# A seventh weight slot for the experts, laid over the constant tables

## The reference

```python
def first_block(x, c, ...):
    ...                                     # attention and gated linear attention
    h = rms_norm(x, g_pre_ffn[l]) * (1.0 + scale2) + shift2
    y = moe_ffn(h, router_w[l], router_b[l], w_gate_up[l], b_gate_up[l], w_down[l], b_down[l])
    return x + gate2 * rms_norm(y, g_post_ffn[l])

def moe_ffn(h, router_w, router_b, w_gate_up, b_gate_up, w_down, b_down):
    logits = (xt @ router_w + router_b).astype(jnp.float32)
    top_v, top_i = lax.top_k(logits, TOP_K)            # 4 of 32 experts for each token
    gates = jax.nn.softmax(top_v, axis=-1)
    ...
    gu = xb @ w_gate_up[e] + b_gate_up[e]               # 1024 x 2048 for each expert
    act = x_glu * jax.nn.sigmoid(SWIGLU_ALPHA * x_glu) * (x_lin + 1.0)
    return act @ w_down[e] + b_down[e]                  # 1024 x 1024 for each expert
```

## Time and profile before

| | us |
|---|---|
| median of 3 runs | 2546.22 |
| lowest, highest | 2543.89, 2552.05 |
| the profiled execution | 2542.5 |
| its span | 2540.5 |
| TensorE busy | 2288.7 (90%) |
| VectorE busy | 872.3 (34%) |

### The profile page before, as it was taken

One profiled execution on the slowest core, in us unless ns is written; L12 is line 12 of the kernel. 1 busy time (PEld: TensorE's weight loads), 2 busy tenths in 40 slices (PEclk: granted clock), 3 DMA queues, 4 the chain that ended last, 5 costly groups with the idle time before them and its releaser, 6 DMA issues. The chain is left out here.

```text
span 2540.5 us, 25065 instructions
## 1 busy us (share of the span) xinstructions
PE 2288.7 (90%) x9740; PEld 1310.2 (52%) x9740; DVE 872.3 (34%) x1800; ACT 416.9 (16%) x897; POOL 106.9 (4%) x74
## 2 busy tenths in 40 slices
PE   7999999888898888888879998898789999989998
PEld 4555343333333333333337677655648764647873
DVE  5665222111121122221236434654567301343201
ACT  1222110111111111111122321112321001222100
POOL 1000000000000000000000000000200000000000
PEclk8999999999999999999989999989989999999999
DMA  9766588999989999999977711465246543423441
GB/s 327 272 234 232 195 307 320 412 409 408 372 312 413 412 404 409 409 411 398 402 303 273 262 62 49 171 246 213 100 141 240 188 159 122 161 89 119 165 153 46
DMA packets 212253, 655.47 MB, mean 258 GB/s; under 512 B 8518, under 2 KB 13182, under 8 KB 195540
## 3 DMA queue, kind: packets, MB, share of 16 engines
q1 hardware_dynamic: 208368, 647.86, 67.2%
q0 software_dynamic: 1712, 3.60, 0.4%
q10 hardware_dynamic: 2004, 1.67, 0.2%
HBM read 652.05 MB, written 1.05 MB: 257 GB/s over the span
## 5 line engine op out<-in xcount | busy, mean ns | idle before, releaser
L1599 PE MATMUL ps<-w,XE 128*64 128x512 f32 x1536 | 365.9, 632 | 61.0 <-DMA w<-in_w_gate_up 57.5
L807 PE MATMUL ps<-HF,w 128*128 128x256 f32 x1408 | 309.6, 383 | 1.8 <-DVE CF L2897 1.8
L807 PEld LDWEIGHTS ps<-HF,w 128*128 128x128 f32 x1408 | 270.3, 192 | 41.6 <-issue 4.5
L1599 PEld LDWEIGHTS ps<-w,XE 128*64 128x64 f32 x1536 | 123.5, 145 | 289.0 <-issue 287.4
L1629 DVE TENSOR_TENSOR T<-ps,BB 128x512 f32<-128x512 f32 x64 | 44.3, 692 | 615.5 <-PE ps L1599 615.5
L625 DVE SCALAR_TENSOR_TENSOR AUX<-w,CS,AUX 128x512 f32<-128x512 f32 (+1 forms) x228 | 169.8, 745 | 8.1
L823 PE MATMUL ps<-w,AF 128*128 128x512 f32 x352 | 151.6, 593 | 1.8 <-DVE AF L2919 1.8
L807 PE MATMUL ps<-HT,w 128*128 128x256 f32 x640 | 148.2, 391 | 5.5 <-DVE dqk L2338 3.7
L1670 PE MATMUL ps<-GR,AT 128*64 128x512 f32 x256 | 121.3, 630 | 30.5 <-DMA AUX<-in_w_down 29.8
L823 PE MATMUL ps<-w,HT 128*128 128x512 f32 (+1 forms) x352 | 146.7, 571 | 0.3 <-DVE S L1444 0.3
L1670 PE MATMUL ps<-w,AT 128*64 128x512 f32 x512 | 119.9, 611 | 20.1 <-DMA w<-in_w_down 16.8
(11 more groups left out here) (580 smaller groups left out, 2570.3 us busy)
## 6 DMA issues: line engine op xcount, KB each, us to landing
w<-in_w_gate_up SPq DMA_DIRECT2D x96, 2048.0 KB, 15.8
w<-in_w_down SPq DMA_DIRECT2D x32, 2048.0 KB, 19.4
w<-in_ada_w SPq DMA_DIRECT2D x24, 2048.0 KB, 8.0
w<-in_ffn_w_in SPq DMA_DIRECT2D x20, 2048.0 KB, 8.0
w<-in_w_in SPq DMA_DIRECT2D x17, 2048.0 KB, 9.7
GR<-in_w_gate_up SPq DMA_DIRECT2D x16, 2048.0 KB, 18.2
AUX<-in_w_gate_up SPq DMA_DIRECT2D x16, 2048.0 KB, 23.0
GR<-in_w_down SPq DMA_DIRECT2D x16, 2048.0 KB, 10.1
```

What stands on the lines that cost most here:

```text
L807: ins = e.matmul(out_, w[:, k, c:c + n], HT[:, k, :], start=k == 0, stop=k == kc - 1, skip_group_check=True)
L1599: ins = e.matmul(b[j * n:j * n + n, :], FM.XE[:, side(x), 4 * kh + k, j * n:j * n + n], ring.tile(512, 1024, "gu", ex_, h, kh, x[0])[:, k, ...
```

## The change

A third region becomes a weight slot in the experts. CT and SEL become one tensor `tables`, and its columns 512 to 4607 are slot 6. The constants that the experts read are moved into the first 512 columns (iota and SU go ahead of the others). The new slot is opened by ("gla", "out", 1), which is counted at L1433. `Ring.use` puts slot 6 first in the turn, ahead of the four that go on, and slots 4 and 5 at the end. Behind the experts `tables_again` loads columns 512 to 3711 and SEL again, between the fourth and the fifth of the second block's loads; TensorE waits for it before L2388 and VectorE before its attention.

```diff
@@ const_table
     c["ones"] = np.ones((128, 128))
+    c["iota"] = np.broadcast_to(np.arange(128)[None, :], (128, 128))
+    c["SU"] = p < f
     c["U64"] = (p <= f) & same
...
@@ Ring.use
-        self.turn, self.k = turn + [s for s in range(n) if s not in turn], 0
+        new = [s for s in range(n) if s not in turn]
+        self.turn, self.k = new[2:] + turn + new[:2], 0
@@ Ring.fetch
         elif i >= 4:
-            e.wait_ge(*first)
+            e.wait_ge(*first[i])
@@ memory
+KEPT = 512
...
-    m.CT = sb("CT", [128, max(b for _, b in const_table()[0].values())])
-    m.SEL = sb("SEL", [8, 1024])
+    n_ct = max(b for _, b in const_table()[0].values())
+    tables = sb("tables", [128, n_ct + 1024])
+    m.CT, m.SEL = tables[:, 0:n_ct], tables[0:8, n_ct:]
...
-    m.SLOTS = [w[:, :] for w in m.W] + [m.GR[:, 1:5, :].rearrange("p a n -> p (a n)"), m.AUX[:, :]]
+    m.SLOTS = [w[:, :] for w in m.W] + [m.GR[:, 1:5, :].rearrange("p a n -> p (a n)"), m.AUX[:, :], tables[:, KEPT:KEPT + 4096]]
@@ moe_sync
-        ring.use(6)
+        ring.use(7)
+        opened = {4: at("rows used"), 5: at("rows used"), 6: at("gla", "out", 1)}
         for x in PAIRS:
-            pair_sync(e, x, at("rows used"))
+            pair_sync(e, x, opened)
@@ second_sync
+    def tables_again(e):
+
+        for sem, v in at.leavers(*ring.user[6]):
+            e.wait_ge(sem, v)
+        e.dma_start(CT[:, KEPT:], T["consts"][:, KEPT:]).then_inc(sems["tables_landed"], 16)
+        e.dma_start(m.SEL, T["sel"]).then_inc(sems["tables_landed"], 16)
+
...
             ring.load(e, wi2[:, c:c + width], 1024, width, name)
+            if n == 1:
+                tables_again(e)
@@ second_pe, second_dve
         b = bank.take(e, "gc")
+        e.wait_ge(sems["tables_landed"], 32)
...
+        e.wait_ge(sems["tables_landed"], 32)
         attention_dve(e, "att2", F2, lambda t: C(f"CB{t}"), PT2, lambda t: F2.O[:, t, 512:1024])
```

More of the change, by code:

```diff
@@ L36, in const_table @@
     c["LF"] = p >= f
-    c["SU"] = p < f
     c["B64"] = same
@@ L56, in const_table @@
         c[n + "q"] = v * 0.125
-    c["iota"] = np.broadcast_to(np.arange(128)[None, :], (128, 128))
     t = np.arange(256)[None, :]
@@ L87 @@
 NV = -(-NV // 128)
-SEMS = ("psum_ready", "scalar_written", "vector_written", "gpsimd_written", "first_consts_landed", "consts_landed", "x_landed",
+SEMS = ("psum_ready", "scalar_written", "vector_written", "gpsimd_written", "first_consts_landed", "consts_landed", "tables_landed", "x_landed",
         "vectors_of_act_landed", "vectors_of_pool_landed", "rows_landed", "gate_lr_landed", "glr_landed", "router_landed", "bias_rows_landed",
@@ L1472, in start_sync @@
         e.dma_start(CT[:, 256:], T["consts"][:, 256:]).then_inc(sems["consts_landed"], 16)
-        e.dma_start(m.SEL[:, :], T["sel"]).then_inc(sems["consts_landed"], 16)
+        e.dma_start(m.SEL, T["sel"]).then_inc(sems["consts_landed"], 16)
         for i, src in enumerate((T["b_mod"][0, 3072:4096], T["b_mod"][0, 4096:5120], T["g_pre_ffn"][0, :])):
```

## The result

| | before | after |
|---|---|---|
| median, us | 2546.22 | 2520.72 |
| lowest to highest, us | 2543.89 to 2555.89 (5 runs) | 2515.68 to 2534.37 (5 runs) |
| the profiled execution, us | 2542.5 | 2534.4 |

The ratio is 0.9892, with an interval of 0.9866 to 0.9917. Of 2546.2 us that is a gain of 27.5 us, between 21.1 and 34.1. The two medians taken alone differ by 25.5 us. The forecast gain was 20.3. The profiled execution of after is the slowest of its five, so its own time against the earlier trace rows's execution (8 us less) says little, and the stages have to be read one by one.

A forecast was written before the change was run, and what follows sets the result against it. Experts bound by transfers at 410 GB/s in most stretches, by TensorE in two where the DMA pauses for slots. −5.6 − 1.7 − 13.0 + 0 = −20.3 us from the median 2546.2 gives 2526; range 2520 to 2539.

The forecast's parts named there:

- The first pair's wait and its clock: First pair's down tiles: the 4.40 us wait and two smaller go, −5.6; the lower clock behind it goes, −1.7.
- The two hand-overs: Where TensorE's pace gives way to the transfers', up to about 410 and 690 to 755 us: 6.6 and 6.4, −13.0.
- the start that was added: At each hand-over, a transfer's start after a pause, at most 3.2 us beyond the 5.1 us tile; some 1.4 taken.
- In between, nothing more is gained: Experts from about 430 to 690 and 770 to 1299 us: DMA already full, so no gain there.
- the rival in which the stream gets slower: Stretches at the DMA's pace: each transfer takes longer, deciding from 0.12 us a tile; at 391 GB/s 2567 us; chance 0.04.
- The rival that all waits are for want of slots: TensorE's waits for experts' tiles: a slot could free up to 104.1 us, giving 2442; chance 0.01.
- The reload: Tables loaded again behind the second block's fourth load: hidden, 0, or 4.0 us if uncovered; rival of a visible reload, 0.08.
- The distance to the mask's matmul: Behind the experts, from the last step to L2388: stays as it was.

The follow-up runs named there:

- the reload alone: The change with six slots in the experts, keeping merged tensor, moved columns, reload and its two waits, against the kernel before: 2552.64 us, 1.0001.
- the first part: Seven slots for the tiles of pairs 0 to 3 only, six from pair 4 on, against the kernel before: 2539.41 us, 0.9951.
- the repeat: The changed kernel run once more without an edit, for a second trace, against the kernel before: 2526.95 us, 0.9906.

## Why the prediction was right and where it failed

**The first pair's wait and its clock: right.** The wait of 4.40 us is gone, and the clock behind it is 1.00 where it was 0.81. A control stands in the kernels with six slots there (the reload alone, seven from pair 8, seven from pair 4): they have the wait and 0.81, 0.81 and 0.83, and every kernel with seven there has neither. The Trainium skill, "TensorE: Matmul & The Clock Gate" (HAM oscillation), has a DMA wait throw the engine back to its lower clock; this trace agrees here, 4.4 us of idleness with 0.81 behind it and none with 1.00. By pair 2 the gain was 8.8 against 7.3. Of the 1.5 us more, 0.9 are there ahead of the wait: the down tiles' step starts at 312.15 where it started at 313.04.

**The two hand-overs: right in place, 2 us too large.** The forecast had 6.6 and 6.4; measured are 5.1 from pair 2 to pair 3 (13.9 − 8.8) and 5.8 from pair 3 to pair 8 (19.7 − 13.9). These are one tile of 5.1 and little of the start that was added, so the upper bound of 3.2 us for a start was nearly all too much. That pair 8 came out even, 19.7 against 20.3, is in part luck: the first term was 1.5 too small and these two 2.1 too large.

**"In between, nothing more is gained": the step that failed.** It took the DMA as full on the strength of a share of 1.02 at 410 GB/s in 1000 to 1200 us. The counter-evidence was there, 391 GB/s at a share of 0.99 in the next hundred us; about a third of what is missing there against 413 is the transfers' end, the rest are pauses. The prediction put that down to a rate that isn't fixed, and used it only for the rival in which the stream gets slower. It was pauses, and the seventh slot takes them away: 4.2 us in pairs 8 to 15, shown alone by the kernel that has the slot only there. With them the experts end 23.9 and 24.7 us earlier in the two traces of the change, against 20.3. What the first comparison has over that, up to 27.5, is scatter. The rival that all waits are for want of slots named this kind of gain and priced it at up to 104 us; the truth was a small part. Of that rule in the Trainium skill, "Perfetto Trace Analysis" (Optimization Strategy), that the same gap repeating can mean too few buffers, the prediction said that the DMA share denies it. The runs show this half right: the share hid 4 of the 24 us, and yet 99.7 us of such waits are still there with the slot.

**Why the fuller stream gave 4.2 us and not more.** The rows are the first 460 us of the transfers of pairs 8 to 15, before and after.

```profile
803.00:1263.00 460.00, 397.30 (x1780) 158.17 (x1782) 85.55 (x181) 53.16 (x121) 36.75 (x16) 0.95 1.02 407
783.30:1243.30 460.00, 390.53 (x1795) 156.56 (x1794) 88.04 (x187) 53.71 (x122) 36.78 (x16) 0.97 1.02 412
```

5 GB/s more over 460 us are 5.6 us. But the last 8 us of the experts' transfers run at 279 and then 166 GB/s after, and before only the last 4 us are slow (233). Some of what a fuller stream gains is thus given back at its end, I think because the 16 engines have drifted apart and the slowest ends the last tile. This is worked out from the stretches and wasn't tested apart.

**Seven slots from pair 4 on: a clock that fell otherwise.** This kernel gained 14.8 us by its median and 14.0 in its trace's experts, where the forecast's term is 6.4. Its start of pair 8 is 9.1 us nearer to that of pair 3 than before (803.15 − 482.53 = 320.6 against 329.7), while the whole change brings 5.8 there. Most of the difference is one step, the first of pair 6, just ahead of the second hand-over. Before and in this kernel, the step and the first matmul behind it:

```profile
669.20 9.72 PE L1599 MATMUL ps<-w,XE 128*64 128x512 f32 x32 [3.57 <-DMA w<-in_w_gate_up]
678.85 3.79 PE L1735 MATMUL ps<-PG,XN 128*128 128x64 f32 x32
```
```profile
667.02 0.61 PE L1604 MATMUL ps<-w,XE 128*64 128x512 f32 x1 [2.03 <-DMA GR<-in_w_gate_up]
...
674.04 3.79 PE L1740 MATMUL ps<-PG,XN 128*128 128x64 f32 x32
```

The step takes 9.65 us before, 9.75 in after (behind a wait of 3.82), and 7.02 here, where the wait is 2.03. The granted clock of the 16 us around it is 0.79, 0.79 and 1.00. So 2.7 of the 9.1 us are this clock, which here goes with the shorter wait, and 6.4 are left for the hand-over. By the traces the two parts of the experts bring 17.5 + 14.0 = 31.5 us, the whole 24 to 25. Of these 7 us too many, 2.7 are this step, 1.7 are pairs 8 to 15 of the first part (494.5 us against 496.2, with six slots in both), and 1.2 are the start of this kernel's pair 3, up to which it has six slots as before (482.53 against 483.69). The rest wasn't followed. It is one trace of each, so this stands as worked out and not as repeated.

**The reload: right.** SP's issues after, behind the experts, to be compared with the earlier trace rows:

```profile
1292.08 7.20 SPq L195 DMA_DIRECT2D w<-in_w_in  x1
1299.33 5.25 SPq L2173 DMA_DIRECT2D tables<-in_consts  x1
1304.62 0.63 SPq L2174 DMA_DIRECT2D tables<-in_sel  x1
1308.41 0.39 SPq L195 DMA_DIRECT2D w<-in_ada_w  x1
1319.95 0.37 SPq L195 DMA_DIRECT2D w<-in_w_in  x1
```

The fifth load is issued 23.9 us earlier than before, as much as the experts ended earlier. It takes 16.1 us to land in place of 11.5, so it lands 4.6 later, the 4.0 of the byte count and a little more; the sixth lands some 3 us later. Neither is waited for: from 1299 to 1420 us neither TensorE nor VectorE shows a wait for a weight tile, and the kernel with the reload alone measures no cost. The distance to the mask's matmul was forecast unchanged, and in after it is 3 us longer. The change isn't the cause: the repeat lacks the 3 us, and they go with after's lower clock, by these rows of before, after and the repeat, from the last step to that matmul:

```profile
1306.50:1425.00 118.50, 105.28 (x444) 82.36 (x445) 74.70 (x143) 38.11 (x78) 2.36 (x4) 0.93 0.74 266
```
```profile
1282.50:1404.00 121.50, 108.07 (x445) 85.01 (x445) 74.71 (x143) 37.91 (x78) 2.36 (x4) 0.90 0.76 273
```
```profile
1281.80:1400.00 118.20, 105.04 (x444) 82.26 (x445) 74.70 (x143) 38.10 (x78) 2.36 (x4) 0.93 0.78 281
```

The repeat has the reload and the length of before.

**The footing: weak.** The sum was laid on a median of three runs, 2546.2. Over 29 more runs before's median is 2553.2, and after came out at 2520.7 and at 2526.95. That the second is the forecast 2526 is luck: 20.3 from 2553.2 would be 2533. The range ended at 2520, since its largest gain was 23.9 and some scatter. After's 2520.7 lies at that edge, and 0.9892 of 2546.2, which is 2518.7, beyond it. The forecast gain is some 4 us short, the 4.2 of the failed step. The rival of a slower stream counted 165 tiles in the full stretches; 154 land there, and its threshold would be 0.13 us a tile in place of 0.12. Nothing hangs on it: with seven slots a tile took 5.1 us.

## What to carry to other kernels

Read "the DMA is full" from GB/s in short stretches against the best rate of the same kernel, and not from a share that rounds to full: 406 against 413 GB/s was a stream with pauses in it, and one more buffer took them away. A further buffer is worth one transfer at each place where the pace goes from the engine to the stream, and something in the stream as long as issues come little more than one transfer ahead of the landing before (here 3.4 to 6.2 us at 5.1 us a transfer; issues 7 us ahead left the stream full). Compare stages between profiles: the change's experts repeated to 0.8 us in two executions whose totals differed by 11.

## What the hardware showed beside

- The stretch behind the experts, the same instructions in every kernel, took between 1234 and 1250 us over nine profiled executions. Its length goes with the granted clock that it got, 0.95 at 1234 us (before), 0.94 at 1250 (after). This is over half of the gain studied, and one kernel gave 1250 and 1240.
- A tile of 2 MB took its place in the stream, 5.1 us (492.0 / 96), where every issue came 7 us or more before the one ahead had landed. With five slots, where the second, sixth and tenth tile of each pair are issued 0.1 to 3.4 us before that landing, a tile took 5.7 us on average (551.1 / 96).
- The fourth load behind the experts holds SP for 7.20 us and the tables' for 5.25, though neither waits for a slot. The DMA is full meanwhile (394 and 387 GB/s at a share of 1.05), so in this kernel several large loads in a row cost the issuing engine time as well.
